# A decoder layer's mixers and output projection: two loops through memory, or one unrolled stretch

## The reference

```python
# gated linear attention: 4 heads, d_k=64, d_v=128, chunks of 64 tokens
b = cumsum(g);  o_inter = (q * exp(b)) @ S                      # from the state
scores = causal(q . k . exp(b_i - b_j));  o = o_inter + scores @ v
S = exp(b_last) * S + (k * exp(b_last - b)).T @ v
o = rmsnorm_per_head(o) * silu(r)
# position mixer: 4 groups of 128 channels, 128-token chunks
s_out = gelu(u) * (tril(w_s) @ layernorm(gelu(vs)) + b_s)
mix = concat(o, s_out) @ w_out;  x = x + rmsnorm(mix)           # 1024x1024
```

## Time and profile before

| what | value |
|---|---|
| time, median of 3 runs (range) | 2897.72 us (2897.57 to 2899.57) |
| the profiled execution, span from first to last instruction | 2902.5 us |
| constants for the mixers, 532.7 to 557.9 us of the span | 25.2 us |
| mixers, 557.9 to 813.9 us | 256.0 us |
| output projection, 813.9 to 1039.4 us | 225.5 us |

### The profile page before, as it was taken

How to read it: one execution, slowest core, us unless ns; L and a number is a source line. 1 busy time by engine, 2 the same in 40 slices (tenths; PEclk the granted TensorE clock), 3 DMA queues, 4 the chain that set the end, 5 groups by cost and what they waited for, 6 DMA issues and landing times. The chain is left out here.

```text
span 2902.5 us, 37010 instructions
## 1 busy us (share of the span) xinstructions
PE 2687.5 (93%) x13396; PEld 2426.7 (84%) x13396; DVE 1041.1 (36%) x1619; ACT 874.4 (30%) x1718; POOL 523.1 (18%) x626
## 2 busy tenths in 40 slices
PE   7999999477779969999999999999799999996998
PEld 5789999455568869999999999999678888885887
DVE  4200000277743254444444444444422242323332
ACT  4311111133331254333333333333422242223332
POOL 2100000154522431111111111111000003221222
PEclk9999999677789979999999999999899999998999
DMA  4211221644434441111111111111354476643221
GB/s 145 90 62 67 69 69 62 158 111 127 113 112 130 140 158 44 52 41 47 57 38 49 44 47 55 38 49 45 125 155 117 118 216 190 190 131 121 77 78 48
DMA packets 305867, 274.77 MB, mean 95 GB/s; under 512 B 17398, under 2 KB 267782, under 8 KB 305766
## 3 DMA queue, kind: packets, MB, share of 16 engines
q1 hardware_dynamic: 305804, 273.94, 30.8%
HBM read 188.11 MB, written 85.78 MB: 94 GB/s over the span
## 5 line engine op out<-in xcount | busy, mean ns | idle before, releaser
L1385 PE MATMUL up_acc<-xh,up_wh 128*128 128x416 f32 x1760 | 620.3, 352 | 0.0
L1385 PE MATMUL up_acc<-xl,up_wh 128*128 128x416 f32 x1760 | 617.0, 351 | 0.0
L1385 PE MATMUL up_acc<-xh,up_wl 128*128 128x416 f32 x1760 | 616.7, 350 | 0.0
L1312 DVE SCALAR_TENSOR_TENSOR up_conv<-up_up,ffn_features,up_conv 128x416 f32<-128x416 f32 (+1 forms) x440 | 284.0, 645 | 570.5 <-ACT up_conv L1229 558.3
L1385 PEld LDWEIGHTS up_acc<-xh,up_wl 128*128 128x128 f32 x1760 | 330.4, 188 | 4.1
L1385 PEld LDWEIGHTS up_acc<-xl,up_wh 128*128 128x128 f32 x1760 | 331.2, 188 | 2.7
L1385 PEld LDWEIGHTS up_acc<-xh,up_wh 128*128 128x128 f32 x1760 | 330.2, 188 | 2.7
L1689 PE MATMUL down_acc<-down_wh,down_sh 128*128 128x512 f32 x748 | 293.8, 393 | 23.1 <-DVE down_sl L1620 23.1
L1223 ACT ACTIVATE up_up<-up_acc 128x416 f32<-128x416 f32 (+1 forms) x220 | 113.0, 514 | 606.7 <-PE up_acc L1385 606.7
L1689 PE MATMUL down_acc<-down_wh,down_sl 128*128 128x512 f32 x748 | 293.0, 392 | 0.0
L1689 PE MATMUL down_acc<-down_wl,down_sh 128*128 128x512 f32 x748 | 293.0, 392 | 0.0
(11 more groups left out here) (266 smaller groups left out, 4318.1 us busy)
## 6 DMA issues: line engine op xcount, KB each, us to landing
down_raw<-hidden SPq DMA_DIRECT2D x34, 1408.0 KB, 7.6
hidden<-up_conv SPq DMA_DIRECT2D x110, 208.0 KB, 1.9
up_raw<-in_w_up SPq DMA_DIRECT2D x44, 512.0 KB, 3.9
proj_features<-in_outs SPq DMA_DIRECT2D x65, 208.0 KB, 1.9
down_ahead<-in_w_down SPq DMA_DIRECT2D x40, 256.0 KB, 5.1
in_raw<-in_w_in SPq DMA_DIRECT2D x19, 512.0 KB, 4.2
out_raw<-mix SPq DMA_DIRECT2D x17, 512.0 KB, 4.8
ple_x<-x SPq DMA_DIRECT2D x17, 512.0 KB, 4.3
```

The costliest lines, as they stand in the source:

```text
L1312: last = nc.vector.scalar_tensor_tensor(out=out, in0=x(c), in1=out, scalar=taps[:, at, c:c + 1].rearrange("p a c -> p (a c)"), op0=ALU.mul ...
L1385: last = nc.tensor.matmul(acc[b][:, 0:TB], w[kind][:, k, :], x[:, k, b * TB:(b + 1) * TB], start=(k == 0 and p == 0), stop=(k == KC - 1 an ...
```

## The change

The three stages become one, `phase_mix`, without a hardware loop. Step t of 19 holds the mixers of tile t and the projection of tile t-2, whose 48 matmuls are cut in four parts of 12 between the mixers' pieces. Finished mixer rows stay in the tile `mixed`; the tensor `mix` and its stores and loads go. Heads of a pair go to the two 64-row halves of the array with no zeros between; scores are made per chunk, 64x64, for two heads and two chunks on four quarters of the array; the products of scores and values go to the two halves by chunk. The head norm's mean is made of a rounded square and its rest (two float32r matmuls in place of one float32; POOL makes the rest, L1151, from two ACT passes over the outputs). DVE's state advance is one instruction per head pair instead of two instructions for all. The sample mixers stand whole in steps 0 and 1, ahead of the first projection, and w_out is split there too. The projection's two accumulators are single now, not double.

The diff, cut to its core. Two of PE's new functions:

```diff
+            def make_scores(t):
+                for q in range(2):
+                    for c in range(NCH):
+                        for f in range(2):
+                            chunk = slice(c * C, c * C + C)
+                            last = nc.tensor.matmul(ks_acc[f][chunk, 2 * P + q * C:2 * P + (q + 1) * C],
+                                                    k_in[s][head_rows(f), q, chunk], q_in[s][head_rows(f), q, chunk],
...
+            def within_chunk(t, crossed):
+                for q in range(2):
+                    for c in range(NCH):
+                        f, chunk = (1 - c if crossed else c), slice(c * C, c * C + C)
+                        last = nc.tensor.matmul(o_acc[f][:, q * P + c * C:q * P + (c + 1) * C],
+                                                v[s][chunk, h * DV:(h + 1) * DV], scores[chunk, f, q, :],
...
```

PE's steps:

```diff
+            for t in range(LAST):
+                if mixes(t + 1):
+                    gate_logits(t + 1)
+                if mixes(t):
+                    turn_keys(t)
+                    make_scores(t)
+                    mix_positions(t)
...
+                if projects(t - 2):
+                    project(t - 2, 0, range(0, 4))
+                if mixes(t - 1):
+                    average_squares(t - 1)
...
+                if projects(t - 2):
+                    project(t - 2, 0, range(4, KC))
+                if mixes(t):
+                    make_kv(t)
+                    if t >= 1:
+                        pe.wait_ge(gla_outs, t * 4 - 2)
+                    within_chunk(t, False)
...
+                    from_state(t, 0)
+                if projects(t - 2):
+                    project(t - 2, 1, range(0, 4))
+                if mixes(t):
+                    pe.wait_ge(outputs, t * 2 + 1)
+                    within_chunk(t, True)
...
+                if projects(t - 2):
+                    project(t - 2, 1, range(4, KC))
+                if mixes(t):
+                    pe.wait_ge(states, t * 4 + 2)
+                    from_state(t, 1)
```

POOL's steps:

```diff
+            for t in range(LAST + 1):
+                if projects(t - 3):
+                    row_powers(t - 3)
+                if mixes(t - 1):
+                    split_squares(t - 1)
+                if mixes(t):
+                    open_mixed(t)
+                if mixes(t + 1):
+                    v_scale(t + 1)
+                if projects(t - 3):
+                    add_rest(t - 3)
+                if mixes(t + 1):
+                    make_keys(t + 1)
+                    v_tail(t + 1)
```

DVE's steps:

```diff
+            for t in range(LAST + 1):
+                if projects(t - 3):
+                    scale_rows(t - 3)
+                if mixes(t):
+                    mask(t)
+                if t == 0:
+                    sample_mask()
+                if mixes(t + 1):
+                    v_stats(t + 1)
+                if mixes(t):
+                    add_bias(t)
+                if mixes(t + 1):
+                    log_decays(t + 1)
+                    v_norm(t + 1)
+                if mixes(t - 1):
+                    finish_gla(t - 1)
+                if mixes(t + 1):
+                    make_queries(t + 1)
+                if t < 2:
+                    for k in range(4 * t, 4 * t + 4):
+                        split_w(k)
...
+                if projects(t - 1):
+                    splits(t - 1)
+                if mixes(t):
+                    advance(t, 0)
+                    advance(t, 1)
```

More of the change, by code:

```diff
@@ new lines, in mix_positions @@
+            def mix_positions(t):
+                pe.wait_ge(v_gained, t * 2 + 2)
+                if t == 0:
+                    pe.wait_ge(spatial_cut, 1)
+                    pe.wait_ge(rows_copied, 2)
+                if t >= 1:
+                    pe.wait_ge(biased, t)
+                for h in range(HS):
+                    last = nc.tensor.matmul(m_acc[:, h * P:(h + 1) * P], vn[t % 2][:, h * P:(h + 1) * P],
+                                            m.spatial[:, h, :], start=True, stop=True)
+                last.then_inc(spatials, 1)
@@ new lines, in within_chunk @@
+            def within_chunk(t, crossed):
+                s = t % 2
+                for q in range(2):
+                    for c in range(NCH):
+                        f, chunk = (1 - c if crossed else c), slice(c * C, c * C + C)
+                        h = 2 * q + f
+                        last = nc.tensor.matmul(o_acc[f][:, q * P + c * C:q * P + (c + 1) * C],
+                                                v[s][chunk, h * DV:(h + 1) * DV], scores[chunk, f, q, :],
+                                                start=(not crossed and q == 0), stop=True, skip_group_check=True)
+                if crossed:
+                    last.then_inc(crossed_made, 1)
@@ new lines, in from_state @@
+            def from_state(t, c):
+                s, chunk = t % 2, slice(c * C, c * C + C)
+                for q in range(2):
+                    for f in range(2):
+                        last = nc.tensor.matmul(o_acc[f][:, q * P + c * C:q * P + (c + 1) * C],
+                                                state[c][head_rows(f), q, :], q_state[s][head_rows(f), q, chunk],
+                                                start=False, stop=True, skip_group_check=True)
+                last.then_inc(outputs, 1)
@@ new lines, in project @@
+            def project(o, h, chunks):
+                s = o % 2
+                if chunks[0] == 0 and h == 0:
+                    pe.wait_ge(split, o + 1)
+                if chunks[0] == 0 and o >= 1:
+                    pe.wait_ge(finished, (o - 1) * 2 + (h + 1))
+                if chunks[0] == 0 and o == 0 and h == 0:
+                    pe.wait_ge(s_outs, 6)
+                    pe.wait_ge(s_kv_added, SEQS)
+                for k in chunks:
+                    if o == 0 and h == 0:
+                        pe.wait_ge(w_ready, k + 1)
+                    for p, (xx, ww) in enumerate(((sh, wh), (sh, wl), (sl, wh))):
+                        last = nc.tensor.matmul(acc[h][:, :], xx[s][:, k, :], ww[:, k, 512 * h:512 * h + 512],
+                                                start=(k == 0 and p == 0), stop=(k == KC - 1 and p == 2))
+                if k == KC - 1:
+                    last.then_inc(summed, 1)
@@ L2435, in build @@
     vs_s = dram("proj_vs", [T, HS * P])
-    mix = dram("mix", [D, T])
     x1, x2 = dram("x1", [T, D]), dram("x2", [T, D])
```

1606 lines of the change are left out of this document (754 added, 852 removed).

## The result

The changed kernel takes 2874.73 us (median of 4 runs, 2873.61 to 2877.71), the old one beside it 2898.64 us: a ratio of 0.9914, 95% interval 0.9900 to 0.9928. It is faster, by 24 us. The forecast was 109 us faster, and the time lies outside its range.

What follows compares the result with a forecast made beforehand. Bound: the old mixers' chain, 256 us for 16 tiles, the projection standing apart. Start 92 + 14 steps x 18.8 + projections 33 + tail 9 = 397 us against 506.7, so 109 less: 2789 us, range 2752 to 2842.

Steps and rivals of the forecast that it cites:

- What bounded the old kernel: Old mixers' stage: one chain through four engines, 256 us for 16 tiles, with PE waiting 60.0 us for DVE's state advance.
- PE's work in a step: Steady step: small groups 5.3 us at full clock, with the projection's 10.9 us together 16.2 us.
- halves that don't overlap: Rival, divided groups on PE: no overlap, ten shape changes cost 1.8 us; step 22.2 us, time 2836 us; chance 0.15.
- The wait in the middle: Ahead of L816 in a steady step: PE waits 1.3 us for DVE's first two products, 10.7 against 9.4 us.
- layer norm 1.11: DVE's layer norm, within the 10.7 us path to the products PE waits for: priced at 1.11 us.
- POOL and DVE set the step: Rival: they slow each other, POOL lengthens to 17 us, PE waits at the position mixer; step 20 us, 2805; chance 0.13.
- The clock: Steady step, middle and head: falls of PE's granted clock cost 1.3 us a step, between 0 and 3.1.
- The start: From the stage's start through its first two steps: 92 us, between 75 and 105.
- 17 us of round trips: First two steps: round trips with PE, ACT and SP on top of DVE's work, 17 us, between 0 and 30.
- The end: After step 15: three projections, 33 us, and the old tail of 9.0 us, together 42 us.
- The slow rival: Rival: small groups keep PE's granted clock at 0.50; step 31 us, stage 596 us, time 2987 us; chance 0.06.
- signs listed: New profile: stage 397 us, steps 17.5 to 19, idle only before L816, clock above 0.85, step 2 at 92 us.

Runs made afterwards that it cites:

- the last experiment on them: Against the changed kernel with DVE's head products ahead of the layer norm (2805.25 us): all matmuls of four divided groups on one row half; 2821.93 us.
- residual last: Against the changed kernel: POOL adds the residual of tile t-3 behind its keys and last layer norm steps instead of ahead; 2846.15 us.
- all edits: Changed kernel with DVE's head products first, loads before store, sample stores last, start reordered, sample products in step 0's wait, two more end accumulators; 2766.49 us.
- both orders: Against the changed kernel: head products ahead of the layer norm on DVE; POOL does layer norm steps, keys, then residual; 2836.84 us.

## Why the prediction was wrong

**What bounded the old kernel: right.** The wait for the state (60.0 us in the earlier trace rows) is gone from the steady steps; the gain is of the kind foreseen, and under a quarter of its size (24 us for 109).

**PE's work in a step: near.** 16.2 us were counted; where PE never waits a step is 17.2. The groups with rows in the old kernel were right (key-value products 0.60, the mean 0.45), and the unseen ones close: 0.50 and 0.54 in the middle, 0.59 for the two later ones, against 0.45. Most of the rest is in the changes of shape: in most parts of the projection the first matmul takes some 0.1 us more to the next start, and the last as much to the next group, 11.6 us for the four parts instead of 10.9. By this difference the changes cost some 0.7 us there (an estimate), not the 1.8 of the rival; that rival (halves that don't overlap) fell, the halves being worth 0.45 us a group by the last experiment on them.

**The wait in the middle: the step that failed.** The text put DVE's path at 10.7 us against PE's 9.4. The changed kernel has 13.8 (846.30, the last matmul, to 860.09) against 10.0. The wrong term is "layer norm 1.11": it measured 3.99. That duration was taken from a row of the old kernel in which POOL was idle, and carried to a place where POOL's list, which the text itself added up to 12.7 us, puts the residual and the keys beside it. The gating went the same way (1.60 for 1.27). With 1.11 the path is 10.9 us and the wait 0.9, near the forecast's 1.3: the sum was sound, the price of one instruction was that of another neighbourhood.

The rival "POOL and DVE set the step" had the mechanism ("they slow each other where both work") but priced it as POOL being slowed by a third, looked for the wait at the position mixer, and came to 20 us. No step waits there. DVE was the one slowed, 3.6 times in one group, on a path with 1.3 us too much already.

**The clock: right in kind, half the size.** 1.3 us a step were taken out of 0 to 3.1; it is 2.9, with a wait thrice as long as forecast and a clock that stayed low for some 6 us behind it. Term and wait hang together: without a wait the clock costs nothing (1.00 over 90 us), and behind 1.84 us (residual last) it costs 1.7. 17.2 + 3.8 + 2.9 = 23.9 us is the full step; the 14 average 23.0, the first being 19.2 and the second 22.6.

**The start: 105 for 92, at the top of the term's range.** The constants came as predicted (their transposes end at 561.0, 28.3 us into the stage; 28 was taken). Two things were under-priced within the 17 us of round trips: the state of tile 0 behind all of tile 1's DVE work and four splits (13.0 us of PE's waiting), and the tiny products of the sample rows with their states (64 matmul records), which the text counted on DVE and not on PE (13 us, and DVE waits 10.2 for what stands behind them). Order alone gave 10 us back, and the kernel with all edits starts in 85.

**The end: 54 for 42.** "The projection's two accumulators are single now" stood in the description of the change, and was not priced where no mixers lie between two projections: 7.9 us of waits. Of the other 4 us, some 3 are the low clock behind the first two of them (an estimate: half of the 6 us at 0.50). With both gone the end takes 42.6 us, so the prediction's 42 was right for an end without waits.

**The rest.** The slow rival (2987) is out: the clock was 0.87 in the steady part. Of the signs listed, three came out (idle ahead of L816 alone in a steady step, divided groups under 0.7 us at full clock, a clock above 0.85), and three didn't (397 us, 17.5 to 19 us, 92 us). The stage was 25.4 us shorter in the two profiled executions; the remaining 3.5 us of the difference of their spans lie in the later stages, which the change leaves alone, and the medians differ by 24.

## What to carry to other kernels

A duration from a trace holds for the neighbours it had there. When work of DVE and POOL is put side by side anew, price a DVE instruction that works on SBUF alone up to the end of the POOL instruction running then, and at most its own time more (the layer norm's ended 0.08 us behind POOL's each time), above all on the path to an engine that waits. That is a price on the safe side: not every such instruction was slowed. In a list by hand, the item that frees another engine's accumulators goes ahead of work that is only wanted a step later; and a store that waits in SP's list holds every load behind it, so that delaying the work ahead of a store can cost more than it clears.

## What the runs showed of the chip

- DVE's layer norm instruction of 128x128 took 0.34 us alone and 2.37 us beside a POOL addition of 128x1024 that had started 0.06 us earlier. The head products, which read PSUM, were not slowed (L1343, 0.74 to 0.76 us for two in all of these kernels). Nor was L1279, which works on SBUF alone: it took 0.42 us inside POOL's power of 128x4 (L1159, 1.25 us) as it does with POOL idle; why is open.
- Behind waits of like length at one place the clock fell in some steps and held in others. Between the position mixer and the projection (both orders) it fell to 0.50 behind 2.20 us at 766.13 and held at 1.00 behind 2.28 us at 863.72; of eight such waits of 1.89 to 2.32 us, three were followed by 0.50. Ahead of L816, between small groups, it fell behind all twelve waits of 3.8 us in the changed kernel. What decides it is not shown. The wait at 766.13, and windows behind it and behind the one at 863.72:

```profile
766.13 0.50 PE L846 MATMUL mix_out_acc<-mix_wh,mix_sh 128*128 128x512 f32 x1 [2.20 <-DVE mix_y L1374]
...
767.00:768.00 1.00, 1.00 (x4) 0.81 (x3) 1.00 (x6) 0.00 (x0) 0.00 (x0) 0.50 0.92 332
...
864.00:865.00 1.00, 1.00 (x6) 0.80 (x5) 1.00 (x6) 0.00 (x0) 0.02 (x1) 1.00 0.90 246
```

- Four matmuls of 64 columns on two row halves took 0.50 us at full clock, written in turn or in series, and 0.95 us on one half.
